# A two-block transformer kernel on one core: convolution taps in pieces, turned row sums, and head-norm sums for two tiles in four 64x64 corners

## The reference, cut to what matters

```python
def dwconv(x, w, n_rows):
    ...
    y = xp[:, :, 0:row_len] * w[0]
    for t in range(1, taps):
        y = y + xp[:, :, t:t + row_len] * w[t]
kv = jax.nn.silu(dwconv(p[..., OFF_K:OFF_BA], conv_w[:, :2 * B_WIDTH], 1)).astype(f32)
```

```python
qa = _rmsnorm(hs(a_q, NA_HEADS), q_norm_a)      # likewise ka, cka, qb, kb, ckb
s = jnp.einsum('bqkgd,btkd->bkgqt', q, k).astype(jnp.float32) * (HEAD_DIM ** -0.5)
p = jax.nn.softmax(s, axis=-1).astype(v.dtype)
return jnp.einsum('bkgqt,btkd->bqkgd', p, v)
```

## Time and profile before

| | us |
|---|---|
| median of 3 runs | 2660.03 (2658.13 to 2660.22) |
| the profiled execution | 2660.28, its span 2658.0 |
| PE busy | 2597.2 (98% of the span) |
| DVE busy | 1321.7 (50%) |
| ACT busy | 802.6 (30%) |
| POOL busy | 847.5 (32%) |
| mean granted clock of TensorE | 0.996 |

### The profile page before, as it was taken

The page is one execution under the profiler, slowest core; times in us unless marked ns, Lnnn a source line. Parts: engine busy times, 40 slices in busy tenths (PEclk is TensorE's granted clock), DMA queues, the critical chain, the costliest instruction groups (busy, mean ns, idle before and its releaser), DMA issues.

```text
span 2658.0 us, 40435 instructions
## 1 busy us (share of the span) xinstructions
PE 2597.2 (98%) x15584; PEld 1934.2 (73%) x15584; DVE 1321.7 (50%) x2373; ACT 802.6 (30%) x1683; POOL 847.5 (32%) x716
## 2 busy tenths in 40 slices
PE   6899999999999999999999999999999999999999
PEld 2677777775788878888884567765555567778887
DVE  3455555553356568778842256533224513753334
ACT  4343333332312112222003336632111223563221
POOL 0222222220456524556534212012323043103444
PEclk9899999999999999999999999999999999999999
DMA  6211111113234434444322110001111122101222
GB/s 228 61 45 45 44 38 45 33 33 135 72 143 168 165 111 158 168 179 171 130 88 77 71 50 24 1 32 64 56 56 60 52 83 80 41 2 48 95 80 95
DMA packets 61408, 220.92 MB, mean 83 GB/s; under 512 B 6784, under 2 KB 8960, under 8 KB 60992
## 3 DMA queue, kind: packets, MB, share of 16 engines
q1 hardware_dynamic: 42576, 153.11, 17.0%
q0 software_dynamic: 14656, 56.89, 6.1%
q10 hardware_dynamic: 4016, 8.65, 0.9%
HBM read 214.90 MB, written 2.15 MB: 82 GB/s over the span
## 4 chain that ended last, share of the span: by engine, by line
PE 95%; DVE 2%; ACT 1%; DMA 1%; issue 1%; ACTq 0%; POOL 0%; DVEq 0%; SPq 0%
PE psum L455 92%; PE psum L957 3%; DMA arena<-in_stream 1%; DVE arena L1781 0%; DVE arena L1778 0%; ACTq L1248 0%; DVE arena L1849 0%; PE psum L683 0%; ACT arena L1357 0%; PE psum L646 0%; POOL arena L2665 0%; DVE arena L2008 0%; ACT arena L1535 0%; DVE arena L2045 0%; DVE arena L2344 0%
## 5 line engine op out<-in xcount | busy, mean ns | idle before, releaser
L455 PE MATMUL psum<-arena 128*128 128x256 f32 (+7 forms) x14784 | 2504.1, 350 | 54.9 <-DVE arena L1709 12.6
L455 PEld LDWEIGHTS psum<-arena 128*128 128x128 f32 (+4 forms) x14784 | 1848.7, 170 | 692.4 <-issue 257.5
L2711 POOL TENSOR_TENSOR arena<-arena 128x512 f32<-128x512 f32 (+1 forms) x104 | 134.6, 1294 | 811.6 <-DMA arena<-in_stream 413.9
L1962 DVE TENSOR_TENSOR arena<-psum,arena 128x256 f32<-128x256 f32 (+1 forms) x103 | 47.4, 460 | 281.0 <-PE psum L455 272.4
L1933 DVE SCALAR_TENSOR_TENSOR arena<-arena 128x1024 f32<-128x1024 f32 x128 | 174.3, 1411 | 0.0
L2715 POOL TENSOR_TENSOR arena<-arena 128x512 f32<-128x512 f32 (+1 forms) x104 | 132.3, 1272 | 103.0 <-PE psum L455 97.4
L1968 DVE TENSOR_TENSOR arena<-psum,arena 128x256 f32<-128x256 f32 (+1 forms) x103 | 47.5, 461 | 228.4 <-PE psum L455 228.2
L2722 POOL TENSOR_TENSOR arena<-arena 128x512 f32<-128x512 f32 (+1 forms) x104 | 144.6, 1390 | 36.4 <-PE psum L455 36.1
L2719 POOL TENSOR_TENSOR arena<-arena 128x512 f32<-128x512 f32 (+1 forms) x104 | 135.5, 1303 | 45.2 <-PE psum L455 38.7
L1411 ACT ACTIVATE arena<-psum 128x256 f32<-128x256 f32 (+1 forms) x103 | 42.6, 413 | 305.2 <-PE psum L455 305.1
L1535 ACT ACTIVATE arena<-psum,arena 128x512 f32<-128x512 f32 (+2 forms) x160 | 115.1, 727 | 28.3 <-DVE arena L2350 15.3
(11 more groups left out here) (274 smaller groups left out, 1747.0 us busy)
## 6 DMA issues: line engine op xcount, KB each, us to landing
arena<-in_stream SPq DMA_DIRECT2D x288, 512.0 KB, 3.8
arena<-in_mods POOLq DMA_DIRECT2D x80, 512.0 KB, 5.7
arena<-gc_rows POOLq DMA_DIRECT2D x16, 384.0 KB, 4.6
arena<-in_bias POOLq DMA_DIRECT2D x16, 384.0 KB, 4.4
arena<-in_xT ACTq DMA_DIRECT2D x2, 1024.0 KB, 14.0
arena<-in_conds ACTq DMA_DIRECT2D x1, 1536.0 KB
arena<-arena POOLq DMA_DIRECT2D x4, 384.0 KB, 4.4
out<-arena SPq DMA_DIRECT2D x3, 512.0 KB, 5.9
```

What stands on the lines that cost most here:

```text
L455: return pe.matmul(out, lhsT, rhs, start=start, stop=stop, skip_group_check=True)
L2711: add(sums[0], a21, a22, ALU.add).then_inc(s("wsum"), 1)
```

## The change

1. **Taps in pieces.** The four tap operations of v, in one piece behind level 1, become `value_taps(i, part)`: the first latent tap behind level 0, the second behind level 1, both context taps behind level 2.
2. **Turned sums.** ACT spreads the reciprocal sums along the free dimension into an SBUF buffer (`widen`, behind `exps`), and PE transposes that buffer into bank 7 (`spread`, between `transposes(u - 1)` and `values(u - 2)`): one transpose a unit, two for a context unit. The wait for `to_att` stands before `spread`. DVE's `to_att` also waits for the values.
3. **Four corners.** `head_sums(p)` sums the squares of both tiles of a pair by four 64x64 matmuls, one in each corner of the array; the odd tile's two heads land with their halves exchanged in banks 6 and 7, and `head_root` of an odd tile is split by halves to set them back. It runs once a pair. Roots, squares and scales are ordered anew around it, context keys of layer 1 and the latent values go into other banks, and `last_sum` (tile 12, plain as before) stands between the context chunks and the latent chunks of VB.

```diff
+        inv_sums = arena[:, rsum_at + SEQ + 16 * WIDE:][:, 0:4 * P].rearrange("p (a b) -> p a b", a=2)
...
-                    pe.wait_ge(s("at_ri"), g + u + 1)
+
+                def spread(u):
+
+                    p, q, b = us[u]
+                    pe.wait_ge(s("at_wide"), g + u + 1)
+                    if b == 0 and (g + u):
+                        pe.wait_ge(s("at_att"), att_before(l, p) + q)
                     for b2 in range(CC if q else 1):
-                        for a in range(2):
-                            o = stat(u, a, b2 if q else None)
-                            m = mm(psum[half(a), 7, (b + b2) * P:(b + b2 + 1) * P],
-                                   st[:, 2, o:o + 1].to_broadcast([P, HD]), ident)
-                            if not q or b2:
-                                m.then_inc(s("at_rs"), 1)
+                        m = pe.transpose(psum[:, 7, (b + b2) * P:(b + b2 + 1) * P],
+                                         inv_sums[:, u % 2, b2 * P:(b2 + 1) * P], ident)
+                    m.then_inc(s("at_rs"), 1)
...
                     if u >= 2:
+                        spread(u - 2)
                         values(u - 2)
...
+                def head_sums(p):
+
+                    pe.wait_ge(s("b2_hsq"), 13 * l + 2 * p + 2)
+                    pe.wait_ge(s("b2_hrn"), 13 * l + 2 * p + FREE)
+                    parts = [(4, 6, slice(0, SEQ))]
+                    if wide or 2 * p in CTX_HEADS:
+                        parts.append((5, 7, slice(SEQ, TOK)))
+                    for to, to2, cols in parts:
+                        n = cols.stop - cols.start
+                        for v, bank in ((0, to), (1, to2)):
+                            for h in range(2):
+                                m = mm(psum[side(h if v == 0 else 1 - h), bank, 0:n], ones[side(h), 0:HP],
+                                       hsq[side(h), v, cols])
+                                if cols is parts[-1][2]:
+                                    m.then_inc(s("b2_hsum"), 1)
...
                     def before():
 
-                        head_sum(a - 2)
                         ended(p - 1)
...
+                    if l and p in (1, 2):
+                        pe.wait_ge(s("join"), 3 * qk_at(l, p - 1) + 2)
...
-                        second = lambda: head_sum(a - 1)
+                        second = lambda: head_sums(p - 1)
...
                 last_head(range(2))
-                head_sum(10)
                 ended(QK_PAIRS[l] - 1)
                 last_head(range(2, KT)).then_inc(s("used"), 1)
-                head_sum(11)
+                head_sums(5)
...
+                def widen(u):
+                    o, n = stat(u, 0), CC if us[u][1] else 1
+                    act.wait_ge(s("at_ri"), g + u + 1)
+                    if g + u >= 2:
+                        act.wait_ge(s("at_rs"), g + u - 1)
+                    for b2 in range(n):
+                        v = st[:, 2, o + b2:o + b2 + n + 1:n, None].to_broadcast([P, 2, HD])
+                        m = f(inv_sums[:, u % 2, b2 * P:(b2 + 1) * P].rearrange("p (a d) -> p a d", a=2), v, ACT.Copy)
+                    m.then_inc(s("at_wide"), 1)
...
                     if u < len(us):
                         exps(u)
+                    if 1 <= u <= len(us):
+                        widen(u - 1)
...
-                    snapshots(n, banks[n % 2], snaps2, half_of(l), True, first if p else None,
-                              (lambda: head_root(l, a - 1)) if a else None)
+                    snapshots(n, banks[n % 2], snaps2, half_of(l), True, (lambda: square(a - 1)) if p else None,
+                              (lambda: head_root(l, a - 2)) if a else None)
+                    if a:
+                        head_root(l, a - 1)
                     square(a)
...
+            def value_taps(i, part):
+
+                w0, w2 = vecd("conv", 8 + i), vecd("conv", 56 + i)
+                if part == 0:
+                    dve.wait_ge(s("centre"), 3 * i + 3)
+                    stt(cbv[:, 1:SEQ], psum[:, 6, 0:SEQ - 1], w0, cbv[:, 1:SEQ], ALU.mult, ALU.add).then_inc(s("tap"), 1)
+                elif part == 1:
+                    dve.wait_ge(s("tap"), 5 * i + 4)
+                    stt(cbv[:, 0:SEQ - 1], psum[:, 6, 1:SEQ], w2, cbv[:, 0:SEQ - 1], ALU.mult, ALU.add)
+                else:
...
-                    if l == 1:
-                        outer_taps(i, 2, cbv, 6, 7, 3, 1)
+                    if l < 3:
+                        value_taps(i, l)
...
                     if p:
                         ended(p - 1)
-                        scale(a - 2)
...
                     join_first(n, y, snaps2, KQ[:, a, 0:w], w)
                     if a:
-                        scale(a - 1)
+                        scale(a - 2)
...
                     join_fourth(n, x, snaps2, KQ[:, a + 1, w:2 * w], w)
+                    if a:
+                        scale(a - 1)
```

More of the change, by code:

```diff
@@ L1065, in _ @@
                     mm(psum[:, 1 - qk_at(0, 0) % 2, :], ones, plain_sum).then_inc(s("nsum"), 1)
[L1066 to L1072, removed]
                 def context_keys(p):
@@ L1084, in context_keys @@
                         for k in range(KT):
-                            m = mm(psum[:, 6 + n, 0:CTX], wk[:, k * P:(k + 1) * P], H[:, k, SEQ:TOK], k == 0, k == KT - 1)
+                            m = mm(psum[:, banks[(qk_at(l, p) + 1) % 2][0], CTX * n:CTX * n + CTX], wk[:, k * P:(k + 1) * P],
+                                   H[:, k, SEQ:TOK], k == 0, k == KT - 1)
                     m.then_inc(s("out_part"), 1)
@@ L1123, in _ @@
                 last_head(range(2))
-                head_sum(10)
                 ended(QK_PAIRS[l] - 1)
                 last_head(range(2, KT)).then_inc(s("used"), 1)
-                head_sum(11)
+                head_sums(5)
                 wv = weights(pe, T0 + L_VB)
                 for c in (*range(XC, CH), *range(XC)):
-                    if c == 1:
-                        head_sum(12)
+                    if c == 0:
+                        last_sum()
+                        pe.wait_ge(s("b2_raw"), 13 * l + 13 + FREE)
                     for k in range(KT):
-                        m = mm(psum[:, 2 if c >= XC else 7, (c % 4) * P:(c % 4 + 1) * P], H[:, k, c * P:(c + 1) * P],
+                        m = mm(psum[:, 2 if c >= XC else (3 if l else banks[n % 2][0]), (c % 4) * P:(c % 4 + 1) * P], H[:, k, c * P:(c + 1) * P],
                                wv[:, k * P:(k + 1) * P], k == 0, k == KT - 1)
@@ L1501, in head_root @@
                 w = TOK if both else SEQ
-                act.wait_ge(s("b2_hsum"), 13 * l + j + 1)
+                act.wait_ge(s("b2_hsum"), 28 * l + 4 * (j // 2) + 4)
                 act.wait_ge(s("b2_qk"), 13 * l + max(j - 1, 0) + FREE)
-                m = f(hrn[:, j % 2, 0:SEQ], psum[:, 4, :], ACT.Ln, scale=1.0 / HD, bias=vec("eps"))
-                if both:
-                    m = f(hrn[:, j % 2, SEQ:TOK], psum[:, 5, 0:CTX], ACT.Ln, scale=1.0 / HD, bias=vec("eps"))
+                rows = [(side(h), side(1 - h)) for h in range(2)] if j % 2 else [(slice(0, P), slice(0, P))]
+                for to, at in rows:
+                    m = f(hrn[to, j % 2, 0:SEQ], psum[at, 4 + 2 * (j % 2), :], ACT.Ln, scale=1.0 / HD,
+                          bias=vec("eps")[at])
+                    if both:
+                        m = f(hrn[to, j % 2, SEQ:TOK], psum[at, 5 + 2 * (j % 2), 0:CTX], ACT.Ln, scale=1.0 / HD,
+                              bias=vec("eps")[at])
                 m.then_inc(s("b2_hrn"), 1)
@@ L1583, in _ @@
                     n, a = qk_at(l, p), QK_FIRST[l] + 2 * p
[L1585 to L1591 removed]
+                    snapshots(n, banks[n % 2], snaps2, half_of(l), True, (lambda: square(a - 1)) if p else None,
+                              (lambda: head_root(l, a - 2)) if a else None)
+                    if a:
+                        head_root(l, a - 1)
                     square(a)
+                square(11)
                 head_root(l, 10)
[L1594 removed]
+                square(12)
                 head_root(l, 11)
[L1596 removed]
+                head_root(l, 12)
                 act.wait_ge(s("out_part"), 5 * l + 3)
@@ L1599, in _ @@
                     .then_inc(s("b2_vb"), 1)
-                head_root(l, 12)
                 act.wait_ge(s("used"), T0 + L_VB + 1)
-                f(VBt[:, 0:XC, :], psum[:, 7, :].rearrange("p (a b) -> p a b", a=XC), ACT.Copy).then_inc(s("b2_vb"), 1)
+                f(VBt[:, 0:XC, :], psum[:, 3 if l else banks[n % 2][0], :].rearrange("p (a b) -> p a b", a=XC), ACT.Copy).then_inc(s("b2_vb"), 1)
                 attention(l)
@@ L1782, in outer_taps @@
                 m.then_inc(s("conv"), 1)
+            def value_taps(i, part):
[7 more added lines that the diff above has]
+                else:
+                    stt(cbv[:, SEQ + 1:TOK], psum[:, 7, 0:CTX - 1], w0, cbv[:, SEQ + 1:TOK], ALU.mult, ALU.add)\
+                        .then_inc(s("tap"), 1)
```

(3 more changed lines are left out.)

44 lines of the change are left out of this document (18 added, 26 removed).

## The result

The changed kernel takes 2642.89 us (median of 4 runs, 2641.09 to 2644.19) against 2660.09 (4 runs, 2658.13 to 2660.22) of the kernel before: ratio 0.9939, 95% interval 0.9926 to 0.9951, 17.2 us less. The forecast was 2639.0 with a range of 2633 to 2648. Three edits were meant to bring 24.5 us net of the entry; the stalls that they cause were meant to cost 3.3 and cost about 8.

What follows compares the result with a forecast made beforehand. PE bounds the key and query stage and the attentions, a chain of waits partly over DVE the delta rule; 6.4 + 9.7 + 8.8 - 3.3 - 0.4 = 21.2 us off 2660.28 gave 2639, range 2633 to 2648.

Steps and rivals of the forecast that it cites:

- Taps, -6.4: Delta rule: tap pieces behind three levels remove level 2's excess, 0.8 us a head, 6.4 us over eight heads.
- 1.04 us of idle time: Delta rule: DVE idles 1.04 us between two levels' masks; one latent tap fits there, both context taps just fit.
- Corners, -9.7: Key and query stages: four 64x64 matmuls at once save 0.95 us in eight context pairs, 0.53 in four others, 9.7 us.
- The estimate from four strips of 128x32: Head sums: corners take 1.33 us like four parallel strips, plus 0.3 for shape changes, 1.63 us a context pair.
- Rivals 1, 2 and 3: Head sums: corners two at a time, 2652, chance 0.09; staggered, 2644, 0.06; one after another, 2680, 0.02.
- Turned sums, 0.11 a unit: Attentions, on PE: one transpose replaces four value records, saving 0.11 us a unit, 0.22 a context unit, 8.8 us together.
- Stalls at the ends of near pairs, +3.3: Attentions: widens delay ACT's copy and DVE's `to_att`, so PE waits at nine near-pair ends, 3.3 us lost.
- The fourth near pair and all far ones have margins of 0.8 and more ... and lose nothing: Attentions: at these ends of pairs the later `to_att` was claimed to cost PE nothing, margins 0.8 us and more.
- Entry, +0.4: Entry of layer 0's attention: first maxima start 0.4 us late and PE's fill gap grows by as much.
- the bound of 6: Attentions: upper bound of the stalls at ends of pairs, 6 us if each widen is twice as long.
- Rival 4: Attentions and delta rule: waits eat the turned sums wholly and taps catch up by themselves, 2648 us, chance 0.05.

Runs made afterwards that it cites:

- the early copy: The changed kernel with ACT's copy of the sums at ends of pairs moved ahead of the exponentials, one iteration earlier: 2635.59 us, ratio 0.9908.

## Why the prediction was right, and where not

- *Taps, -6.4*: right. 6.2 in the trace over seven heads, 7.7 (5.1 to 11.2 by its interval) alone. That 1.04 us of idle time takes in a piece and no more was right too; the pieces are 0.74 and, for both context taps, 0.99 (173.48 to 173.99 + 0.48).
- *Corners, -9.7*: right in mechanism and size: -5.6 and -3.9 in the trace, 10.1 alone. The estimate from four strips of 128x32, 1.63 us a pair, was nearly the value itself (1.65). Rivals 1, 2 and 3 fall with the 1.46 us of a group.
- *Turned sums, 0.11 a unit*: right to the hundredth, and free within a pair.
- *Stalls at the ends of near pairs, +3.3*: right in place, small in size. Layer 0's latent ends lose 0.57 each (forecast 0.50), the context blocks 0.32 (0.31), layer 1's 0.38 (0.28): 3.8 us in nine places.
- *"The fourth near pair and all far ones have margins of 0.8 and more ... and lose nothing"*: this is the step that failed. The 0.8 is the margin of `to_att` against `spread`. But `to_att` stands in DVE's queue ahead of the maxima and the eviction, and a far unit's scores wait for that eviction. Two rows of the trace of before that I had not drawn on, values and eviction of that unit in order of time:

```profile
1678.62 1.54 PE L455 MATMUL psum<-arena 128*64 128x128 f32 x24
...
1679.31 0.68 DVE L2358 COPY arena<-psum 128x512 f32<-128x512 f32 x1
```

The values ended at 1680.16 and the eviction at 1679.99: the margin of the true path was 0.17, not 0.8. DVE later by 0.47 and PE earlier by 0.22 leave 0.52 of stall, and the scores start 0.15 behind the eviction's end (1669.35 against 1668.52 + 0.68): 0.67, and 0.70 were measured. Layer 0 has four such ends, those of the fourth near pair and of three far ones; they lost 0.70 three times and 0.98 once, and the fourth near pair of layer 1 lost 0.17: 3.3 us. At the end with 0.98 ACT's exponentials start 0.37 us behind the maxima instead of 0.09, and the copy with them; why stays open.

- *The last context unit*, with no scores behind it, isn't in the forecast: 1.1 us, where the early copy leaves 1.0.
- *Entry, +0.4*: it didn't come. The stretch with the entry lost 5.6, where 5.7 less 0.4 was forecast, and PE's gap ahead of the first transposes is 1.40 us where it was 1.35.

So the stalls came to 3.8 + 3.3 + 1.1 = 8.2 us instead of 3.3, beyond the bound of 6 as well; 4.9 more. The total is 3.9 above the forecast; the difference of 1.0 lies within what taps (1.3) and corners (0.4), each timed alone, and the entry (0.4) brought more than forecast, which the intervals can't make firm. Rival 4 had "a stall of 0.5 also in the far units", which was nearly what happened there, at a chance of 0.05; the turned sums were indeed eaten wholly, while the taps did not catch up by themselves. That the time stayed in the range although the stalls left their bounds is in part luck: the taps and the corners came out at their forecasts or a little better, and the range had room for errors in every term.

## What to carry to other kernels

When work is put ahead of an instruction on an in-order queue, follow everything behind it, on its own engine and on the ones that it releases: the margin is that of the tightest waiter down the list, not of the first one named. A small operation is best placed where its engine waits for something else: one copy moved from behind the exponentials to before them was worth some 7 us, two fifths of what the whole change brought. And a part of a change can be worth nothing alone (here, the turned sums) until the wait that it makes is moved off the path.

## What the runs showed of the hardware

- Four 64x64 matmuls in the four corners run at once, at the starts 7, 13 and 20 ns behind the first, though both row halves of a tile write one PSUM bank, into different partitions: 16 records, 512 and 256 columns, in 1.46 us up to the next plain matmul. By the same measure the four strips of 128x32 took 51.66 - 50.22 = 1.44 with the same columns; the 1.33 of the earlier trace rows stops 0.1 short of the next plain matmul, whose weights are loaded here:

```profile
51.66 0.30 PEld L455 LDWEIGHTS psum<-arena 128*128 128x128 f32 x2 [0.41 <-issue]
```

The rule on banks that the prediction weighed (the Trainium skill, TensorEngine Tiling (Array Packing), Gotcha 1: PSUM Pressure), that matmuls in different row tiles can't use one bank at the same time, does not hold for these float32 matmuls; the measurement decides.

- A reciprocal on DVE costs by what it writes: 934 ns for 128x128, of which only two columns are distinct, 0.16 us for 128x2. The plain copy of the same shape on ACT takes 0.31.
- Of two operations on DVE that follow at once, the second starts 0.08 us before the first ends (170.57 and 169.91 + 0.74); where it has to wait for the first one's result it starts 0.03 to 0.04 behind (171.07 against 170.57 + 0.47).
